# Windowed attention's queries and keys are normed and turned block by block between the projections, values are projected last, and ScalarE empties the projection banks

## What is computed

```python
def prep(t):
    q, k, v = jnp.split(t @ w_in, [D_MODEL, D_MODEL + H_KV * HEAD_DIM], axis=-1)
    return (_rmsnorm(_heads(q, H_ATTN), q_norm_w), _rmsnorm(_heads(k, H_KV), k_norm_w), _heads(v, H_KV))

q, k, v = prep(h)
q, k = rope(q), rope(k)
qc, kc, vc = prep(hc)
# scores of each query block against its window and against all context keys,
# one softmax over both and a sink, times the values, then @ w_out
```

## Time and profile before

| | |
|---|---|
| median of 3 runs | 2460.55 us (2460.31 to 2461.69) |
| the profiled execution, its own time | 2458.4 us |
| its span, first to last instruction | 2456.6 us |
| PE, PEld, DVE, ACT, POOL busy | 94%, 68%, 44%, 17%, 4% of the span |
| mean granted TensorE clock | 0.964 |
| the attention's projections begin, in the span | 897.9 us |
| its first score begins | 984.9 us |
| its output projection begins | 1044.5 us |

### The profile page before, as it was taken

One profiled execution on the slowest core, in us unless ns is written; L12 is line 12 of the kernel. 1 busy time (PEld: TensorE's weight loads), 2 busy tenths in 40 slices (PEclk: granted clock), 3 DMA queues, 4 the chain that ended last, 5 costly groups with the idle time before them and its releaser, 6 DMA issues.

```text
span 2456.6 us, 39259 instructions
## 1 busy us (share of the span) xinstructions
PE 2310.4 (94%) x16956; PEld 1677.2 (68%) x16956; DVE 1082.3 (44%) x2072; ACT 414.3 (17%) x972; POOL 109.2 (4%) x103
## 2 busy tenths in 40 slices
PE   6999998999999997899999889999997889999997
PEld 5444453478885885588887568888774767676765
DVE  2586464478885427834522654440434420000001
ACT  1211151100000021611001031000322221110111
POOL 0210110000002300000000000000003000000000
PEclk8999998999999998999999999999998889999998
DMA  7434522245454141048873225886441257889892
GB/s 276 137 139 157 189 66 69 69 142 201 137 195 119 49 174 39 1 170 277 293 210 130 103 69 195 298 265 178 154 167 40 69 174 290 315 311 340 312 339 103
DMA packets 305672, 427.47 MB, mean 174 GB/s; under 512 B 11539, under 2 KB 166706, under 8 KB 305258
## 3 DMA queue, kind: packets, MB, share of 16 engines
q1 hardware_dynamic: 301456, 419.79, 50.2%
q10 hardware_dynamic: 4058, 5.35, 0.6%
HBM read 423.88 MB, written 1.13 MB: 173 GB/s over the span
## 4 chain that ended last, share of the span: by engine, by line
PE 87%; DVE 8%; ACT 1%; issue 1%; DMA 1%; ACTq 0%; POOL 0%; DVEq 0%; SPq 0%; POOLq 0%
PE banks L594 73%; PE banks L838 3%; DVE mem L1653 2%; DVE mem L1650 1%; PE banks L603 1%; ACT mem L2639 1%; PE banks L1453 1%; PE banks L943 1%; DVE mem L1646 1%; PE banks L673 1%; DVE mem L2163 1%; PE banks L978 1%; PE banks L1301 1%; DVE mem L2217 1%; PE banks L1517 1%
## 5 line engine op out<-in xcount | busy, mean ns | idle before, releaser
L594 PE MATMUL banks<-mem 128*32 128x128 f32 (+4 forms) x12788 | 1855.1, 359 | 34.3 <-ACT mem L2639 12.1
L594 PEld LDWEIGHTS banks<-mem 128*32 128x32 f32 (+2 forms) x12788 | 1334.7, 150 | 535.2 <-issue 323.6
L1650 DVE SCALAR_TENSOR_TENSOR mem<-mem 128x512 f32<-128x512 f32 (+5 forms) x509 | 365.3, 744 | 14.5 <-ACT mem L2639 5.2
L2639 ACT ACTIVATE mem<-mem 128x256 f32<-128x256 f32 (+8 forms) x441 | 191.5, 483 | 785.1 <-DVE mem L1650 537.8
L2639 ACT ACTIVATE mem<-banks 128x512 f32<-128x512 f32 (+7 forms) x323 | 128.2, 421 | 1058.8 <-PE banks L594 755.3
L1653 DVE TENSOR_TENSOR mem<-mem,banks 128x256 f32<-128x256 f32 (+3 forms) x88 | 43.3, 492 | 579.0 <-ACT mem L2639 551.4
L1650 DVE SCALAR_TENSOR_TENSOR mem<-banks,mem 128x256 f32<-128x256 f32 (+7 forms) x258 | 133.7, 543 | 359.6 <-PE banks L594 243.8
L1653 DVE TENSOR_TENSOR mem<-mem 128x256 f32<-128x256 f32 (+12 forms) x279 | 158.7, 579 | 42.0 <-ACT mem L2639 20.2
L1653 DVE TENSOR_TENSOR mem<-banks,mem 128x256 f32<-128x256 f32 (+3 forms) x223 | 93.2, 420 | 142.6 <-PE banks L594 83.8
L603 PE MATMUL banks<-mem 128*128 128x128 f32 (+4 forms) x392 | 64.1, 307 | 35.4 <-DMA mem<-in_gdn_conv_w 13.0
L603 PEld LDWEIGHTS banks<-mem 128*128 128x128 f32 (+4 forms) x392 | 49.2, 159 | 60.6 <-issue 22.5
(11 more groups left out here) (184 smaller groups left out, 906.8 us busy)
## 6 DMA issues: line engine op xcount, KB each, us to landing
mem<-in_ada_w SPq DMA_DIRECT2D x96, 1024.0 KB, 10.5
mem<-in_moe_w_gate_up SPq DMA_DIRECT2D x64, 1024.0 KB, 12.9
mem<-in_ffn_w_in SPq DMA_DIRECT2D x44, 1024.0 KB, 7.0
mem<-in_moe_w_down SPq DMA_DIRECT2D x48, 768.0 KB, 9.5
mem<-in_moe_w_gate_up SPq DMA_DIRECT2D x32, 768.0 KB, 12.7
mem<-in_ffn_w_out SPq DMA_DIRECT2D x32, 704.0 KB, 6.9
mem<-in_ffn_w_gate_up SPq DMA_DIRECT2D x22, 1024.0 KB, 6.6
mem<-in_ab_w_in SPq DMA_DIRECT2D x16, 1024.0 KB, 6.7
```

Source lines behind the costliest of these rows:

```text
L594: ins = nc.tensor.matmul(o, lhsT, rhs, start=start, stop=stop)
L1650: return V.scalar_tensor_tensor(out=o, in0=a, scalar=sc, in1=b, op0=op0, op1=op1)
L2639: ac = lambda o, i, f, **k: nc.scalar.activation(o, i, f, **k)
```

## The change

The queries and keys are no longer normed and turned in phases of their own. The matmuls that sum squares and those that rotate are placed between the projections, two blocks at a time:

- PE: after two query blocks and the projection that follows them, one `square_sum` of 512 columns for the two. After the next pair's sum, the two `rotated` matmuls of the pair before. The keys' sums are two of 256 columns for each block. Values are projected last, all four tiles, with the last sums and rotations of the keys among them. The rotations no longer go through the projection banks but through banks 6 and 7, with semaphores of their own (`att_scaled` before, `rot_taken` for the bank). The item count of the stage falls from 34 to 22, and three counts further on are shifted by 12.
- ACT empties all projection banks: of a query or key block it writes a copy and a square, both from the bank; of a value tile a copy; of a sum the root, with scale 1/64 and the epsilon as a bias. `double_k` makes the eight copies of the turned keys, ahead of the last value tile.
- DVE is left with the reciprocals, now taken of the root and in six pieces of 512 columns, the multiplications, and `rope`. It empties only the banks of the rotations.
- The first score no longer waits for everything: scores 0, 4, 8 and 12 wait for their head's key copies (`kdup_ready`), score 1 for the last use of banks 6 and 7, and the first `weigh` for the last projection bank.

The diff, cut to its core; the lines removed from DVE's program are those told above, L2156 to L2205.

```diff
-NPROJ = {"gdn": 137}
+NPROJ = {"gdn": 125}
...
+        a_eps = a_rs[:, 7, 0:1]
+        two_of = lambda v, b: v[:, b:b + 2, :].rearrange("p a t -> p (a t)")
+        ATT_FIRST = 49
+        ATT_ITEMS = ("q", "q", "q", "sum", "q", "q", "sum", "q", "q", "sum", "q", "k", "sum", "k", "sum_k", "sum_k", "v", "sum_k", "sum_k", "v", "v", "v")
...
-    for _ in range(2):
-        w = panel(8, 512)
-        for b in range(4):
-            project(w, slice(b * P, (b + 1) * P), L)
-    def square_sum(b):
-        await_("square_ready", "sq")
+    assert c["proj"].n == ATT_FIRST
+    def square_sum(first, taken, n=2):
         bank = proj_item()
-        if b < 8:
-            o, i = bank[:, 0:L], a_sq[:, b, :]
-        else:
-            o, i = bank[:, :], a_sq[:, 8 + 2 * (b - 8):10 + 2 * (b - 8), :].rearrange("p a b -> p (a b)")
-        nc.tensor.matmul(o, const("halves"), i, start=True, stop=True).then_inc(s["proj_ready"], 1)
+        pe.wait_ge(s["proj_taken"], ATT_FIRST + taken)
+        i = two_of(a_sq, first) if n == 2 else a_sq[:, first, :]
+        nc.tensor.matmul(bank[:, 0:n * L], const("halves"), i, start=True, stop=True).then_inc(s["proj_ready"], 1)
+    def rotated(n):
+        pe.wait_ge(s["att_scaled"], n + 1)
+        if n >= 2:
+            pe.wait_ge(s["rot_taken"], n - 1)
+        i = a_q[:, n, :] if n < 8 else a_k2[:, n - 8, 0:L]
+        nc.tensor.matmul(PS[6 + n % 2][:, 0:L], const("rot"), i, start=True, stop=True).then_inc(s["rot_ready"], 1)
     w = panel(8, 512)
-    for b in range(8):
-        square_sum(b)
-    for b in range(2):
-        project(w, slice(b * P, (b + 1) * P), T2)
+    for b in range(3):
+        project(w, slice(b * P, (b + 1) * P), L)
+    square_sum(0, 2)
+    project(w, slice(3 * P, 4 * P), L)
+    w = panel(8, 512)
+    project(w, slice(0, P), L)
+    square_sum(2, 5)
+    rotated(0)
+    rotated(1)
+    project(w, slice(P, 2 * P), L)
+    project(w, slice(2 * P, 3 * P), L)
+    square_sum(4, 8)
+    rotated(2)
+    rotated(3)
+    project(w, slice(3 * P, 4 * P), L)
+    w = panel(8, 512)
+    project(w, slice(0, P), T2)
+    square_sum(6, 11)
+    rotated(4)
+    rotated(5)
+    project(w, slice(P, 2 * P), T2)
+    for half in range(2):
+        square_sum(8 + half, 12, 1)
+    rotated(6)
+    rotated(7)
     project_tok(w, 0, slice(256, 512), 256)
-    for b in range(8, 10):
-        square_sum(b)
-    for t in range(1, 4):
-        project_tok(w, t, slice(256, 512), 256)
-    await_("dve_for_pe", "dve")
-    for b in range(10):
-        bank = proj_item()
-        i = a_q[:, b, :] if b < 8 else a_k2[:, b - 8, 0:L]
-        nc.tensor.matmul(bank[:, 0:L], const("rot"), i, start=True, stop=True).then_inc(s["proj_ready"], 1)
-    await_("dve_for_pe", "dve")
+    for half in range(2):
+        square_sum(10 + half, 14, 1)
+    project_tok(w, 1, slice(256, 512), 256)
+    rotated(8)
+    project_tok(w, 2, slice(256, 512), 256)
+    rotated(9)
+    project_tok(w, 3, slice(256, 512), 256)
     def score(n, bank):
+        if n % 4 == 0:
+            pe.wait_ge(s["kdup_ready"], 2 * (n // 4 + 1))
+        if n == 1:
+            pe.wait_ge(s["rot_taken"], 10)
         for j in range(2):
             r = slice(j * HD, (j + 1) * HD)
             last = nc.tensor.matmul(PS[bank + j][:, :], a_q[r, n // 2, (n % 2) * P:(n % 2 + 1) * P],
...
     def weigh(n, bank):
+        if n == 0:
+            pe.wait_ge(s["proj_taken"], ATT_FIRST + len(ATT_ITEMS))
         for t in range(4):
             for j in range(2):
                 last = nc.tensor.matmul(bank[j * HD:(j + 1) * HD, 0:P], a_v[:, t, (n // 4) * HD:(n // 4 + 1) * HD],
...
+    V.memset(a_eps, EPS)
     norm(1, 0, col("norm_w", 16, 8), 2)
+    c["proj"].n += len(ATT_ITEMS)
+    def inverse(n):
+        v = two_of(a_sq, 2 * n)
+        dve.wait_ge(s["att_rooted"], n + 1 if n < 4 else 2 * n - 2)
+        link(V.reciprocal(v, v))
+    def q_scaled(n):
+        inverse(n)
+        for b in (2 * n, 2 * n + 1):
+            stt(a_q[:, b, :], a_q[:, b, :], col("attn_q_norm_w"), a_sq[:, b, :], ALU.mult, ALU.mult).then_inc(s["att_scaled"], 1)
+    def k_scaled(b):
+        inverse(4 + b)
+        stt(a_k2[:, b, :], a_k2[:, b, :], col("attn_k_norm_w"), two_of(a_sq, 8 + 2 * b), ALU.mult, ALU.mult).then_inc(s["att_scaled"], 1)
+    def turned(n):
+        dve.wait_ge(s["rot_ready"], n + 1)
+        dve.wait_ge(s["att_scaled"], n + 1)
+        rope(a_q[:, n, :] if n < 8 else a_k2[:, n - 8, 0:L], PS[6 + n % 2], a_rs).then_inc(s["rot_taken"], 1)
+        dve.wait_ge(s["rot_taken"], n + 1)
+    q_scaled(0)
+    for n in range(3):
+        q_scaled(n + 1)
+        turned(2 * n)
+        turned(2 * n + 1)
+    k_scaled(0)
+    turned(6)
+    turned(7)
+    k_scaled(1)
+    turned(8)
+    turned(9)
     dve.wait_ge(s["phase_loaded"], 32)
     wmask = at(phase0, 2, T2)
...
-    c["proj"].n = 49
-    for b in range(8):
-        act.wait_ge(s["proj_taken"], 49 + b + 1)
-        ac(a_sq[:, b, :], a_q[:, b, :], ACT.Square).then_inc(s["square_ready"], 1)
-    for b in range(2):
-        act.wait_ge(s["proj_taken"], 49 + 16 + b + 1)
-        ac(a_sq[:, 8 + 2 * b:10 + 2 * b, :].rearrange("p a t -> p (a t)"), a_k2[:, b, :], ACT.Square)\
-            .then_inc(s["square_ready"], 1)
-    for b0, b1 in ((0, 4), (4, 8), (8, 10), (10, 12)):
-        root(a_sq[:, b0:b1, :])
+    seen = {"q": 0, "k": 0, "v": 0, "sum": 0, "sum_k": 0}
+    def double_k(b):
+        act.wait_ge(s["rot_taken"], 8 + b + 1)
+        for kv in (2 * b, 2 * b + 1):
+            r = (kv % 2) * HD
+            for half in range(2):
+                ac(a_kdup[half * HD:(half + 1) * HD, kv, :], a_k2[r:r + HD, b, :], ACT.Copy).then_inc(s["kdup_ready"], 1)
+    for n, kind in enumerate(ATT_ITEMS):
+        b = seen[kind]
+        seen[kind] += 1
+        if (kind, b) == ("v", 3):
+            double_k(0)
+            double_k(1)
+        act.wait_ge(s["proj_ready"], ATT_FIRST + n + 1)
+        bank = PS[(ATT_FIRST + n) % 4]
+        if kind == "q":
+            ac(a_q[:, b, :], bank[:, 0:L], ACT.Copy)
+            ac(a_sq[:, b, :], bank[:, 0:L], ACT.Square).then_inc(s["proj_taken"], 1)
+        elif kind == "k":
+            ac(a_k2[:, b, :], bank[:, :], ACT.Copy)
+            ac(two_of(a_sq, 8 + 2 * b), bank[:, :], ACT.Square).then_inc(s["proj_taken"], 1)
+        elif kind == "v":
+            ac(a_v[:, b, :], bank[:, 0:L], ACT.Copy).then_inc(s["proj_taken"], 1)
+        else:
+            v, width = (two_of(a_sq, 2 * b), T2) if kind == "sum" else (a_sq[:, 8 + b, :], L)
+            ac(v, bank[:, 0:width], ACT.Sqrt, scale=1.0 / HD, bias=a_eps).then_inc(s["att_rooted"], 1)
+            act.wait_ge(s["att_rooted"], b + 1 + (4 if kind == "sum_k" else 0))
+            act.nop().then_inc(s["proj_taken"], 1)
     attention(16, 0, weights, T2)
     c["out"].n += 8
...
-        act.wait_ge(s["proj_taken"], 83 + b + 1)
+        act.wait_ge(s["proj_taken"], 71 + b + 1)
```

More of the change, by code:

```diff
@@ L229, in build @@
             "final_copied",
+            "att_rooted", "att_scaled", "rot_ready", "rot_taken", "kdup_ready",
         ):
@@ L2165, in copy_v @@
-                def copy_v(t):
-                    bank = item()
-                    V.tensor_copy(a_v[:, t, :], bank[:, 0:L]).then_inc(s["proj_taken"], 1)
-                def q_normed(b0):
-                    await_("rstd_ready", "rstd")
-                    for b in range(b0, b0 + 4):
-                        stt(a_q[:, b, :], a_q[:, b, :], col("attn_q_norm_w"), a_sq[:, b, :], ALU.mult, ALU.mult)
-                for b in range(8):
-                    bank = item()
-                    scale(a_sq[:, b, :], bank[:, 0:L], 1.0 / HD, EPS).then_inc(s["proj_taken"], 1)
@@ L2177, in _ @@
-                dve.wait_ge(s["proj_taken"], c["proj"].n)
-                for b in range(2):
-                    bank = item()
-                    V.tensor_copy(a_k2[:, b, :], bank[:, :]).then_inc(s["proj_taken"], 1)
-                    inverse(4 * b, 4 * b + 4)
-                copy_v(0)
-                for b in range(2):
-                    bank = item()
-                    scale(sq2(b), bank[:, :], 1.0 / HD, EPS).then_inc(s["proj_taken"], 1)
-                dve.wait_ge(s["proj_taken"], c["proj"].n)
@@ L2187, in _ @@
-                for b in range(2):
-                    copy_v(1 + b)
-                    inverse(8 + 2 * b, 10 + 2 * b)
-                    q_normed(4 * b)
-                copy_v(3)
-                for b in range(2):
-                    await_("rstd_ready", "rstd")
-                    last = stt(a_k2[:, b, :], a_k2[:, b, :], col("attn_k_norm_w"), sq2(b), ALU.mult, ALU.mult)
-                last.then_inc(s["dve_for_pe"], 1)
-                for b in range(10):
-                    bank = item()
-                    dst = a_q[:, b, :] if b < 8 else a_k2[:, b - 8, 0:L]
-                    rope(dst, bank, a_rs).then_inc(s["proj_taken"], 1)
-                    dve.wait_ge(s["proj_taken"], c["proj"].n)
@@ L2201, in _ @@
-                for kv in range(4):
```

(6 more changed lines are left out.)

9 lines of the change are left out of this document (1 added, 8 removed).

## The result

The changed kernel takes 2438.01 us (median of 4 runs, 2436.47 to 2438.51), the one before 2460.43. The ratio is 0.9912, with a 95% interval of 0.9900 to 0.9925: 22 us or 0.9% faster. The forecast was 2440.3 in a range of 2437.5 to 2449, and faster with a chance of 0.93.

The account below looks back on a forecast made before the run. The 23.9 us ahead of the first score were taken to belong to DVE. DVE's first mask 20.4 earlier, less 0.2 for a late exponential, gave 2460.55 - 20.2 = 2440.3 us, range 2437.5 to 2449.

Parts of the forecast that it names:

- What bounded the stage: From the end of the projections to the first score, 960.96 to 984.87, the 23.9 us belong to DVE.
- PE's own work: Projections and sums stay the same; ten rotations between projections cost 0.43 each, and PE is through at 965.4.
- The waits on PE: At sums and rotations between projections: DVE needs 7.0 per pair against PE's 8.6; no wait, 0.1 to spare at rotation 9.
- The walk: Step-by-step times of PE, ACT and DVE through the preparation: second key block's product at 961.5, rotation 9 at 961.6.
- The tail: ACT's last copies, value tile and table load end at 969.4, so the first exponential is 0.6 late.
- the two prices for the table load: Ahead of the first exponential: 1.29 by the profile row, or 2.66 with a 1.38 drain by the Trainium skill.
- It will shift as a whole: The attention behind the preparation starts earlier with DVE's first step, 20.4, and does not get shorter.
- Loss 0.2: In the first attention step DVE needs the exponentials at 970.7 and gets them at 970.9, 0.2 lost.
- A sign of being wrong: Wrong would be a rotation 9 wait over 1, first score behind 968, or over 60 from first score to output projection.
- rival 1: At rotation 9 and ACT's copies, DVE or ACT is slower than priced: 2443.9, twice that 2447.5; chance 0.22.
- Rival 2: Behind the attention the gain is given back at something starting at a fixed time: 2449 to 2460.5; chance 0.06.
- Rival 3: Stops at the rotations lower PE's clock, 45.7 us take twice as long: 2486, slower than before; chance 0.04.

Follow-up runs that it names:

- rotations_last: The changed kernel with the ten rotations and their turns put back in one row behind all projections; 2451.54 us, 0.9967 of the kernel before.
- keys_last: The changed kernel with the value tiles projected ahead of the keys; 2450.04 us.
- dve_empties: The changed kernel with DVE again making the fourteen copies out of the projection banks; 2441.01 us, first score 1.22 later.
- filler: The changed kernel with eight matmuls of unused result in PE's idle stretch between scores 1 and 2; 2441.49 us, mask to output 57.60.
- tail_v1: The changed kernel with last value tile between scores 1 and 2, table load behind the last root, two key copies in steps 3 and 4; 2440.50 us.
- tail_v2: The changed kernel with tail_v1's three edits, and score 0's two key copies made by DVE between turns 8 and 9; 2436.15 us, 0.9907 of before.

## Why the prediction was right

**What bounded the stage.** The prediction said that the 23.9 us from the last value tile to the first score belonged to DVE. rotations_last and keys_last confirm it from two sides: whatever of DVE's chain is no longer beside a projection comes back at DVE's price.

**PE's own work.** First score at 965.4 - 897.88 = 67.5 after the first projection was forecast; 67.39, 67.76 and 67.38 were measured. The ten rotations at 0.43 cost what was said. The forecast of the granted clock, 1.00 until the first score, holds but for the first 4.1 us, which were low before the change too.

**The waits on PE.** None was expected, with 0.1 to spare at rotation 9. Measured was a hold-up of 0.08 there and none elsewhere. The walk said the second key block's product would come 961.5 - 897.88 = 63.6 after the first projection, and it ended at 961.65 + 0.75 = 962.40, 63.25 after; PE was there at 962.49, 63.34 after, where the walk had 63.7. So both were 0.35 earlier than forecast, and the slack of 0.1 stayed. dve_empties showed that lateness at this place counts in full, as written.

**The tail.** DVE's first mask was forecast at 68.8 and came at 68.64; ACT was forecast ready for the first exponential at 71.5 and started it at 970.61 - 899.15 = 71.46. The copies cost 5.19 / 8 = 0.65 each, within the bounds of 0.42 and 0.7, near the 0.6 that I took. The exponential was forecast 0.6 late, of which DVE would feel 0.2. It came 2.82 after DVE's first mask instead of 2.12, 0.70 late, and DVE waited 0.32. Of the two prices for the table load the row's was right: it stands 0.02 behind the copy ahead of it, and the exponential starts 1.30 after its start. The drain of 1.38 that the Trainium skill (ScalarE: Activation LUTs, What ACT_TABLE_LOAD costs) adds does not appear in this place.

**The step that failed.** "It will shift as a whole when DVE's first step starts earlier," and with it the term "Loss 0.2". The attention did not shift as a whole. From the first mask to the output projection it took 59.29, 58.11 and 59.27 in the three profiles, where 57.48 had been. The output projection was forecast at 1024.3 - 897.88 = 126.4 after the first projection and came at 127.93, 127.11 and 127.90. A sign of being wrong that the prediction had named, more than 60 from the first score to the output projection, came true in two of the three: 60.54, 59.35 and 60.52. I had seen that ACT would be late, and priced it by DVE's wait alone. What I left out is that PE waits for the same exponential, 3.67 instead of the 2.39 of the kernel before:

```profile
990.77 1.51 PE L1108 MATMUL banks<-mem 64*128 64x512 f32 x4 [2.39 <-ACT mem L2639]
...
994.28 1.37 PE L1108 MATMUL banks<-mem 64*128 64x512 f32 x4
```

In that wait, or just behind it, the clock falls, and scores 2 and 3, wholly or partly at 1.2 GHz, hold DVE. filler isolates it: 0.5 to 1.7. So the price of the tail was 0.6 to 1.8, not 0.2, and the stage gained 18.7 to 19.6 against the one profile of before, not 20.2.

**The rivals.** The late tail, rival 1, is what happened in a small way, at another spot than it named: not at rotation 9 but behind score 1. Rival 2, a gain given back later, did not happen: the time behind the stage, 1409.62 to 1412.06 in the changed kernel, is not above the 1412.06 of before. Rival 3 named the low clock but put it at the rotations, where PE never stopped.

**The whole time.** It fell by 22.4, 2.2 more than forecast, though the stage gained less than forecast. From the stage alone it would have been 2440.9 to 2441.9. What lies beyond that is not owed to the mechanism. It lies inside the interval of the ratio (18 to 25 us), and the two later groups, where the changed kernel ran beside the one before again, measured 2457.88 - 2440.03 = 17.9 and 2457.86 - 2438.57 = 19.3. So the 22.4 stands at the upper end of the scatter. That the median came out below 2440.3, and not above it, is luck.

## What to carry to other kernels

When DVE owns a stretch in which PE waits, look for the longest chain of small operations per block, and ask where PE has work that needs none of it: here four value tiles and the projections of the next blocks covered 20 us. Put what nobody waits for (the values) last, behind what starts the longest chain (the keys). After such a change look at the first steps of the loop that follows: an idle stretch of PE there has a second price, the clock, and an operation moved into it is free only as long as the stretch stays longer than the operation and the clock stays up. Where the clock matters, repeat the profile of the unchanged kernel before reading a difference below 1 us.

## What the runs showed of the hardware

- The same program had score 2 at 2.08, 1.47 and 2.08 in three executions, each time after 3.67 to 3.68 of idle time. The granted clock fell 3.0 us after PE had stopped in the first and 4.3 us in the second, and was back 6.8 and 3.4 us later. This made 1.2 us of difference in this stage.
- The clock can fall when PE is at work again. In tail_v1 PE stopped for 1.87 and restarted at 963.35, and the clock was at 0.68 in the mean over the 2.77 us that followed. In tail_v2, with 1.46 and 0.25 of idle time, it stayed at 1.00.
- Eight matmuls of no use, in place of 3.67 us of waiting, kept the next scores at 1.13 and made the stage 0.9 to 1.7 shorter.
- A copy of 64x512 from memory to memory took 0.63 on ACT and 0.42 on DVE; eight in a row took 5.19 and 3.47 to 3.59.
- A table load between two activations of ACT cost 1.32 from the end of the one to the start of the next (969.29 to 970.61), of which the load itself is 1.28.
